# RWKV inverse levels 3 and 4 on compact 32-column operands, norms summed in pairs, one modulation chunk moved

## The reference

```
sa = S @ a_t;  S = S*w_t + sa b_t^T + v_t k_t^T;  y = S @ r_t
```

## Time and profile before

| | us |
|---|---|
| median of 3 runs | 2867.43 |
| lowest, highest | 2859.68, 2867.85 |
| profiled execution | 2864.11 |
| its span | 2862.3 |
| TensorE busy | 2540.6 (89%), mean granted clock 0.931 |
| VectorE busy | 889.2 (31%) |
| ScalarE busy | 530.2 (19%) |
| GpSimd busy | 108.5 (4%) |
| HBM read | 664 MB, 232 GB/s over the span |

### The profile page before, as it was taken

How to read it: one execution, slowest core, us unless ns; L and a number is a source line. 1 busy time by engine, 2 the same in 40 slices (tenths; PEclk the granted TensorE clock), 3 DMA queues, 4 the chain that set the end, 5 groups by cost and what they waited for, 6 DMA issues and landing times.

```text
span 2862.3 us, 36896 instructions
## 1 busy us (share of the span) xinstructions
PE 2540.6 (89%) x15550; PEld 1802.8 (63%) x15550; DVE 889.2 (31%) x1581; ACT 530.2 (19%) x1055; POOL 108.5 (4%) x118
## 2 busy tenths in 40 slices
PE   6999989999999899999989999999777777767876
PEld 4757678887758678887658889865333333323433
DVE  2543524301634512222466652331111111111112
ACT  2115411001116311001234432121000000000001
POOL 0100000000100010000011110000000000000000
PEclk9999999999999999999999999999888787888789
DMA  7325547635332364363000001567999999999998
GB/s 307 124 103 235 221 147 297 233 147 206 118 129 92 133 227 158 147 264 114 30 1 1 1 2 60 206 236 302 428 429 428 428 428 428 429 429 429 429 428 366
DMA packets 48786, 666.85 MB, mean 233 GB/s; under 512 B 5530, under 2 KB 5701, under 8 KB 7584
## 3 DMA queue, kind: packets, MB, share of 16 engines
q1 hardware_dynamic: 46656, 656.65, 56.5%
q0 software_dynamic: 2016, 8.53, 0.9%
HBM read 664.11 MB, written 1.05 MB: 232 GB/s over the span
## 4 chain that ended last, share of the span: by engine, by line
PE 65%; DMA 25%; DVE 7%; ACT 2%; issue 1%; POOL 0%; DVEq 0%; ACTq 0%; POOLq 0%
PE bank L2659 52%; DMA ring<-exp_w 21%; PE bank L2667 6%; DMA arena<-exp_w 3%; PE bank L2671 2%; PE bank L2881 2%; DVE arena L2389 1%; PE bank L1869 1%; DMA arena<-x 1%; PE bank L2688 1%; DVE hT L2537 1%; PE bank L1897 1%; ACT hT L2195 0%; ACT arena L2320 0%; PE bank L2901 0%
## 5 line engine op out<-in xcount | busy, mean ns | idle before, releaser
L2659 PE MATMUL bank<-hT,ring 128*128 128x256 f32 (+2 forms) x3232 | 739.1, 388 | 6.3 <-ACT hT L2195 6.3
L2659 PEld LDWEIGHTS bank<-hT,ring 128*128 128x128 f32 x3232 | 607.0, 192 | 138.9 <-issue 63.3
L2667 PE MATMUL bank<-ring,arena 128*32 128x512 f32 (+1 forms) x2496 | 317.5, 650 | 171.1 <-DMA ring<-exp_w 157.0
L2659 PE MATMUL bank<-arena,ring 128*128 128x256 f32 x1600 | 351.5, 382 | 6.7 <-POOL arena L2167 2.8
L2659 PEld LDWEIGHTS bank<-arena,ring 128*128 128x128 f32 x1600 | 304.8, 191 | 50.2 <-POOL arena L2167 3.6
L2667 PEld LDWEIGHTS bank<-ring,arena 128*32 128x32 f32 x2496 | 87.5, 128 | 357.1 <-issue 202.7
L2659 PEld LDWEIGHTS bank<-vec,arena 128*128 128x128 f32 x1344 | 179.9, 215 | 81.1 <-issue 79.0
L2659 PE MATMUL bank<-arena 64*128 64x128 f32 (+4 forms) x1156 | 203.4, 376 | 12.6 <-DVE arena L1417 6.2
L2667 PE MATMUL bank<-arena 128*32 128x256 f32 (+1 forms) x1568 | 162.1, 556 | 43.1 <-DMA arena<-exp_w 42.7
L1610 DVE COPY arena<-bank 128x512 f32<-128x512 f32 x64 | 44.2, 691 | 479.9 <-PE bank L2667 479.9
L2659 PE MATMUL bank<-vec,arena 128*128 128x32 f32 (+2 forms) x1344 | 185.9, 291 | 8.1 <-ACT arena L2200 4.7
(11 more groups left out here) (314 smaller groups left out, 1982.6 us busy)
## 6 DMA issues: line engine op xcount, KB each, us to landing
ring<-exp_w SPq DMA_DIRECT2D x125, 2048.0 KB, 26.3
arena<-exp_w SPq DMA_DIRECT2D x66, 2048.0 KB, 25.9
ring<-w_in SPq DMA_DIRECT2D x38, 2048.0 KB, 7.9
ring<-ada_w SPq DMA_DIRECT2D x24, 2048.0 KB, 7.8
ring<-w_mlp_up SPq DMA_DIRECT2D x16, 2048.0 KB, 7.7
ring<-w_mlp_down SPq DMA_DIRECT2D x16, 2048.0 KB, 7.8
ring<-mod_w SPq DMA_DIRECT2D x12, 2048.0 KB, 7.7
ring<-w_out SPq DMA_DIRECT2D x6, 2048.0 KB, 7.7
```

Source lines behind the costliest of these rows:

```text
L2659: mm = nc.tensor.matmul(out_, a, b, start=(i == 0), stop=(i == len(pairs) - 1))
L2667: mm = nc.tensor.matmul(o, a, b, start=(i < 4), stop=(i >= len(pairs) - 4))
```

## The change

**Norms.** Except for the first norm and that of the context, x is squared in pairs of 256-column tiles as soon as their residual is there, and TensorE does the mean in pairs: after the first half of the last `wo` jobs (or after `down` 5, 6 and 7), the last pair in `norm`. The small modulation matmuls of the gap come after the first `qk` or `up` columns. Modulation chunk 9 of layer 1 (used in layer 0's MLP gap) moves to turn 14 of layer 0, in the attention of kind B.

**Levels 3 and 4.** X^T is kept compact: for a matrix, only the 32x32 diagonal blocks, side by side as 128 partitions x 32 columns; 16 matrices are 128x512. `widen` is masked in 16 pieces of 32 partitions, VectorE turns the compact array in 32x32 blocks, and level 2's T goes. W and XT multiply 128x128 by 32 columns, two tiles per bank. W's mask spreads the result to block-diagonal 128x128. XT of level 3 is copied by ScalarE and turned by VectorE; XT of level 4 is spread by four VectorE masks, and T of level 4 and level 5 are as before. GpSimd makes a masked copy of M for level 3 (32x32 blocks). The order of the steps is new.

```
-NCONST = C_MASKB + 2 * 768
+C_BLOCKS32 = C_MASKB + 2 * 768
+NCONST = C_BLOCKS32 + 128
...
-    own = {0: {10: [0, 1], MLP_NORM: [9, 10, 11]},
+    own = {0: {10: [0, 1], 14: [9], MLP_NORM: [10, 11]},
...
 rwkv_steps, for g in range(4), after the change:
+        if g == 1: NT g 0, NT g 1
+        if old:    S0 q 0, BK q 0, U0 q 0
+        if g != 1: NT g 0, NT g 1
+        if g == 0: mix ctx 8
+        if ahead:  lora n
+        if old:    BK q 1
+        pick g;  if old: U q 0
+        spread g 0;  if old: (q >= 2: Y q 0), S q 0, S0 q 1
+        spread g 1;  if old: U0 q 1, U q 1
+        widen g 0..3;  if g == 0: mix ctx 10;  if old: (q >= 2: Y q 1), S q 1
+        W g 3 half 0, 1
+        n == 1: vt 0;  n == 2: kraw 1, ksq 1
+        AK g 0;  if g >= 2: RB g 0, RB g 1
+        XT g 3 half 0, 1
+        n == 2: kk 1, kinv 1
+        if ahead: scan n
+        AK g 1;  n == 1: mix lat 4
+        W g 4 half 0, 1
+        if ahead: centre n
+        n == 1: mix lat 6;  n == 2: vt 1;  if g >= 2: RK g 0, RK g 1
+        XT g 4 half 0, 1
+        n == 2: kwide 1
+        T g 4 tile 0..3
+        if ahead: exp n
+        W g 5 tile 0..3
+        n == 1: mix lat 8, mix lat 10
+        if ahead: km n, mul n
+        XT g 5 tile 0..3;  T g 5 tile 0..3;  W6, XT6 as before
...
+        def spread_blocks(v):
+            return blocks(v).unsqueeze(2).to_broadcast([P, 4, 4, 32])
+        def block_mask(at):
+            return blocks(const(at)).unsqueeze(1).to_broadcast([P, 4, 4, 32])
...
 GpSimd, after g_add of the unit matrix:
+                    pool.wait_ge(unit_added, 4 * (g + 1))
+                    for tile in range(4):
+                        g_mask(mt32_of(tile), mt_of(tile), rep(const(C_BLOCKS32), 4)).then_inc(masked_32, 1)
...
 ScalarE:
-                elif what == "XT":
+                elif what == "XT" and at[0] == 3:
+                    copy((what, g, *at), compact_xt(g)[:, 256 * at[1]:256 * at[1] + 256], 256)
+                elif what == "XT" and at[0] == 5:
                     copy((what, g, *at), xt_of(g, at[1]), shape=P)
...
 VectorE:
+                elif what == "W" and at[0] < 5:
+                    b = filled(dve, (what, g, *at))
+                    for n, tile in enumerate(tiles_of(at[1])):
+                        last = v.tensor_tensor(four_blocks(w_of(tile)), spread_blocks(b[:, P * n:P * n + P]),
+                                               block_mask(C_OFF + P * (at[0] - 3)), ALU.mult)
+                    free(last, (what, g, *at))
+                elif what == "XT" and at[0] == 3:
+                    emptied(dve, (what, g, *at))
+                    part = slice(256 * at[1], 256 * at[1] + 256)
+                    v.transpose(compact_x[:, part], compact_xt(g)[:, part]).then_inc(x_turned, 1)
+                elif what == "XT" and at[0] == 4:
+                    (as W, into xt_of(g, tile), with C_BLOCKS32)
...
 widen:
+                    to = blocks(compact_xt(g)[:, P * at[0]:P * at[0] + P])
+                    for n in range(4):
+                        part = slice(32 * n, 32 * n + 32)
+                        last = v.tensor_tensor(to[part], rows(b[part, :], P)[:, :, part],
+                                               rep(cst[part, C_EIGHTS + 32 * n:C_EIGHTS + 32 * n + 32], 4), ALU.mult)
+                    free(last, (what, g, *at))
+                    if at[0] == 3:
+                        emptied(dve, (what, g, 3))
+                        v.transpose(compact_x, compact_xt(g)).then_inc(x_turned, 1)
...
 TensorE:
+                elif what == "W" and at[0] < 5:
+                    lev, half = at
+                    b = start((what, g, *at))
+                    pe.wait_ge(x_turned, 3 * g + (1 if lev == 3 else 2 + half))
+                    for n, tile in enumerate(tiles_of(half)):
+                        if lev == 3:
+                            pe.wait_ge(masked_32, 4 * g + tile + 1)
+                        for p in range(CT):
+                            o = P * n + 32 * p
+                            mm = product(b[:, o:o + 32], [(mt32_of(tile)[:, p], blocks(compact_x)[:, 4 * tile + p])])
+                    finish(mm)
+                elif what == "XT" and at[0] < 5:
+                    (the same with w_of(tile)[:, p] and blocks(compact_xt(g))[:, 4 * tile + p])
...
 norms, ScalarE:
-                emptied(act, ("wo", l, 3))
+                for i in range(4):
+                    emptied(act, ("wo", l, i))
+                    square_of_pair("mlp", i)
...
+                for i in range(4):
+                    emptied(act, ("down", l, 2 * i + 1))
+                    square_of_pair("mix" if l + 1 < DEPTH else "lat", i)
...
 norms, TensorE:
                 for i in range(4):
                     w = chunk(("wo", l, i // 2))
+                    b = start(("wo", l, i))
+                    for j in range(2):
+                        if j and i >= 2:
+                            mean_of_squares("mlp", l, range(2) if i == 2 else range(2, 4))
+                        (the columns of half j)
+                    finish(mm)
+                mean_of_squares("mlp", l, range(4, 6))
                 norm("mlp", l)
                 modulations(side_modulations(l, MLP_NORM))
-                modulations([])
...
                 for i in range(16):
                     (up columns i)
+                    if i == 0:
+                        modulations([])
```

More of the change, by code:

```diff
@@ L330, in rwkv_steps @@
             yield "S0", q, 1
-        if new:
-            yield "spread", g, 1
+        yield "spread", g, 1
         if old:
             yield "U0", q, 1
-        if old:
             yield "U", q, 1
[L337 to L343, removed]
+        for tile in range(4):
+            yield "widen", g, tile
+        if g == 0:
+            yield "mix", "ctx", 10
         if old:
@@ L347, in rwkv_steps @@
             yield "S", q, 1
-        for tile in range(4):
-            yield "T", g, 2, tile
+        for half in range(2):
+            yield "W", g, 3, half
+        if n == 1:
+            yield "vt", 0
+        if n == 2:
+            yield "kraw", 1
+            yield "ksq", 1
+        yield "AK", g, 0
+        if g >= 2:
+            yield "RB", g, 0
+            yield "RB", g, 1
+        for half in range(2):
+            yield "XT", g, 3, half
+        if n == 2:
+            yield "kk", 1
+            yield "kinv", 1
@@ L350, in rwkv_steps @@
+        if ahead:
+            yield "scan", n
+        yield "AK", g, 1
+        if n == 1:
+            yield "mix", "lat", 4
+        for half in range(2):
+            yield "W", g, 4, half
         if ahead:
             yield "centre", n
+        if n == 1:
+            yield "mix", "lat", 6
         if n == 2:
[L353 to L375, removed]
-                yield ("exp", "km", "mul")[lev - 3], n
-            if g >= 2 and lev in (3, 4):
-                yield ("RB" if lev == 3 else "RK"), g, 0
-                yield ("RB" if lev == 3 else "RK"), g, 1
-            for tile in range(4):
-                yield "XT", g, lev, tile
-            if lev == 4 and n == 2:
-                yield "kwide", 1
-            for tile in range(4):
-                yield "T", g, lev, tile
-            if lev == 3 and n == 2:
-                yield "kk", 1
-                yield "kinv", 1
-            if lev == 4 and n == 2:
-                yield "exp", n
@@ new lines, in rwkv_steps @@
+            yield "vt", 1
+        if g >= 2:
+            yield "RK", g, 0
+            yield "RK", g, 1
+        for half in range(2):
+            yield "XT", g, 4, half
+        if n == 2:
+            yield "kwide", 1
+        for tile in range(4):
+            yield "T", g, 4, tile
+        if ahead:
+            yield "exp", n
+        for tile in range(4):
+            yield "W", g, 5, tile
+        if n == 1:
+            yield "mix", "lat", 8
+            yield "mix", "lat", 10
+        if ahead:
+            yield "km", n
+            yield "mul", n
@@ L391, in rwkv_steps @@
+        for tile in range(4):
+            yield "XT", g, 5, tile
+        for tile in range(4):
+            yield "T", g, 5, tile
         for ci in range(2):
@@ L589, in second_block @@
             elif what in ("U", "XT", "T", "W6", "pick"):
-                add((what, g, *at), "s")
+                add((what, g, *at), "v" if what == "XT" and at[0] == 4 else "s")
             elif what in ("spread", "widen"):
```

115 lines of the change are left out of this document (78 added, 37 removed).

## The result

| | before | changed kernel |
|---|---|---|
| median, us | 2864.51 (4 runs) | 2932.55 (4 runs) |
| lowest, highest | 2859.68, 2867.85 | 2924.25, 2943.98 |
| profiled execution, us | 2864.11 | 2943.98 |
| TensorE, mean granted clock | 0.931 | 0.900 |

The account below looks back on a forecast made before the run. The prediction took TensorE to bound the kernel until about 2000 us, then expert loads. Inverse +4 and clock +27, less norms 15, gave +16: 2880 from the profiled 2864.1, forecast as 2883 us because that execution lay below the median; range 2852 to 2908.

Parts of the forecast that it names:

- A quarter of the columns costs the same: Levels 3 and 4: passes with 32 moving columns take 0.114 us each, like 128, so W and XT win nothing.
- Rival (b): Narrow passes cost less, say 0.06 us, while the clock still falls: 2869, no change; 0.18 together with a mild Rival (a).
- The clock, +27: Inverse, levels 3 and 4: narrow streams after 3 us of idleness bring half clock, costing 7, 10, 6 and 4 us.
- all at half clock: Inverse: the 32-column passes of levels 3 and 4 and AK wholly at half clock, 16 us per group, 64 in all.
- Rival (a): The clock holds in the inverse because AK, RB and RK break the narrow stretches: 2856, faster; chance 0.25.
- Full clock, net +4, bounds -10 to +14: Inverse at full clock: VectorE's added work and waits against saved transposes, +7, +1, -1 and -3 us by group.
- Rival (c): VectorE bounds the inverse more widely and narrow parts run at half clock nearly throughout: 2911; 0.15 together with Rival (d).
- The turn, 0.65: Inverse, ahead of level 3: VectorE's block transpose of the whole compact X takes 0.65 us, near a mask.
- Norms, -15, bounds 9 to 19: MLP norms of both layers and layer 1's mixer norm: 2.8, 5.2 and 7.0 us faster, 15 in all.
- Rival (d): Loads behind the modulation chunks set the norms' ends, which give only 9 us: 2889; 0.15 together with Rival (c).
- The weights behind the chunks: Layer 0's MLP norm: "up" weights, behind two chunks instead of three, are issued when "wo" ends, at 422.8.
- The sum: Whole kernel: inverse +31 (+4 and +27), norms -15, so +16 on the profiled 2864.1 us; forecast 2883 us.

Follow-up runs that it names:

- wide_streams: The changed kernel with each matmul of W and XT in levels 3 and 4 streaming its 32 columns four times (128 moving columns); 2898.34 us, ratio 1.0127.
- wide_filled: wide_streams with extra 512-column matmuls where TensorE stood idle in the inverse; 2900.93 us, ratio 1.0138.
- the ladder: Kernel before, then adding norms (2857.73 us), order of steps (2862.98), compact operands streamed as 128 columns (2898.34), 32 moving columns (2932.55).
- wide_short_widen: wide_streams with widen masked by one operation per bank instead of four, three of four column blocks left out; 2885.52 us, ratio 1.0075.
- norms_no_move: The kernel before with the new norms and later small modulation matmuls, but chunk 9 kept in layer 0's MLP gap; 2861.00 us, ratio 0.9989.
- narrow_before: The kernel before with only 32 of 128 moving columns in the W and XT products of levels 3 and 4; 2912.12 us, ratio 1.0158.
- order_only: The kernel before with the new norms and the new order of the inverse's steps, but the old full 128-column operands; 2862.98 us, ratio 0.9999.

## Why the prediction was wrong

- **A quarter of the columns costs the same: right.** 3.76 for 32 passes at full clock, 7.01 at half; I had 3.65 and near 7. Rival (b), cheaper narrow passes, is out.
- **The clock, +27: right in mechanism, too small.** It was to be half in each W of level 3 and until T4 in g=0 and 1. It was, but for W of level 3 in g=3, which ran in 3.76. The size was mis-set: I had 7, 10, 6 and 4 us for the four groups, and by the changed kernel's trace the same matmuls took 15.4, 24.8, 14.5 and 17.5 longer. Their sum, 72, is above even my 64 for "all at half clock", because the half clock goes on beyond the products: in g=1 it covers NT(1) and the state products too. With the 32-column streams taken away (wide_streams) only 34.8 us come back: 24 of the 72 stay, as 105 us are still at half clock there, and 13 turn into waits. Rival (a), the clock holds, is out. Even with most of the clock back (wide_filled, 0.90 in the inverse) the change was slower, 2901 and not 2856.
- **Full clock, net +4, bounds -10 to +14: the step that failed most.** wide_streams is 43.5 us over before in the inverse. That is 33.6 of idle time and 24.3 of slower matmuls less 14.4 of transposes. The 24.3 can't simply be taken off: wide_filled has most of the clock back (65 us at half clock, before 37) and is still 40 over, as a faster TensorE only waits longer. Part of these 40 can be the extra matmuls themselves, and no run gives the clock back without adding work, so the term's size stays open between 19 (43.5 less 24.3) and 40. Either is outside its bounds. By the ladder 10.7 of the 43.5 is the order, 34.1 the compact operands (with the 14.4 already taken off), and -1.3 the norms' other start. I had counted VectorE's added work as 4.8 per group; it is 7.6 (203.3 busy, not 172.7, over four). The largest part of that miss that I can name is the 16 small masks: 4.85, where I took 3.4 from a 112-element operation less an overlap that they don't have. And I held VectorE to be the bound in g=0 only, since in the earlier trace rows it is busy for 32.6 and 34.4 of 45.1 and 44.4 us. But those busy shares hid that its masks now stand between a product and the next in every group: wide_short_widen gave back its 15 us one for one. The 2 us that I had in g=0 for GpSimd's extra masks over the spread steps fit: TensorE waits 6.4 for the last spread step there, before 4.3.
- **Rival (c)**, "VectorE is the bound more widely, and half clock nearly throughout", with 2911, had the right shape and was 22 short.
- **The turn, 0.65:** 0.71 for 512 elements, 0.45 for 256. Right.
- **Norms, -15, bounds 9 to 19:** -9.6 by the trace up to the inverse, and 6 in the medians. The root ended when predicted. The step that failed is what the next columns wait for behind the modulation chunks. The three gaps were to give 4.2, 4.6 and 5.3 and gave 2.7, 3.1 and 3.7. In layer 0's MLP I let the weights set "up", at 430.6; the norm's own tail of reciprocal, scaling and shift set it, 1.4 later. In the other two I had no wait at all, and TensorE waits 1.36 and 1.12. Chunk 9 cost 2.9 in the attention, where I had 2.7. The clock gave about 3 of the 3.6 that I had counted, but not where I had put it: behind the MLP norm of layer 0 some 1.9 are lost, as half-clock stretches stand there in the changed kernel too, and 3.3 come from the stretch at 1190 us, which I had not counted. Rival (d), the loads set the norms' ends, had 9, near the mark, but for a reason that the trace shows in one gap only (1.36 for `w_in`): that was luck.
- **The weights behind the chunks:** right, as norms_no_move shows: with a third chunk ahead they come 7 us late.
- **The sum:** -6 for the norms, +5 for the order, +35 for the compact operands at 128 columns, +34 for the 32-column streams: 68, by the medians of the ladder. The forecast had -15, +4 and +27.

The Trainium skill's page "TensorE: Matmul & The Clock Gate", section "HAM oscillation — how this bites in real kernels", puts the loss of the clock down to idle gaps of TensorE. In narrow_before there is no more idle time than before (15.8 and 17.8), and the clock fell in a stretch that was busy throughout: the measurement decides, and narrow streams lose it too. Idle gaps do as well, as the 3.81 us ahead of NT(1) in order_only show.

## What to carry to other kernels

Where each matmul loads its own 128x128 stationary operand, going from 128 to 32 moving columns saved nothing here (3.84 and 3.76 for 32 passes) and cost the granted clock. Repeating the columns gave 34 us back; folding the work so that fewer operands are loaded was not tried. Before trusting a sum of TensorE's savings, lay the other engine's written order beside it: a share of busy time well under one does not say that its queue is off the path. Take changes apart in a ladder before keeping them: here a part worth 6 us was buried under parts that cost 75. And where two costs overlap, as the clock and VectorE's masks do here, taking one away tells its worth only beside the other (15 us in wide_streams, 29.5 in the changed kernel).

## What the hardware showed unexpectedly

- VectorE masks of 32 partitions x 128 elements took 0.30 each in a row of 16 (4.85 in all); of 128 partitions x 128 elements, four took 0.88, or 0.22 each. With a quarter of the partitions an operation took no less.
- A product of 32 passes with its own stationary operands nearly doubles when the clock halves, 3.76 to 7.01, although few columns stream: the 32 loads of the stationary operand take 3.65 at full clock and 6.90 at half.
